# The last product of a hybrid decoder block in another order: low part of the weights first, second token block in two column halves, last squares by quarters

## The chip, the cores and the metric

One NeuronCore of a Trainium2 chip runs the kernel. The metric is the device time of one execution in microseconds (us); a comparison uses the median of several runs. Engines are named as in the profile: PE is TensorE (PEld its weight loads), DVE is VectorE, ACT is ScalarE, POOL is GpSimd, SP is SyncE. "SPq" and "ACTq" are the queues from which SP and ACT issue DMA transfers.

## What is computed

The reference takes 512 tokens of width 1024 through one block: an RMS norm, one input projection, a short gated convolution and a sliding-window attention side by side, both gated and merged, an output projection with residual, then a second norm and a squared-ReLU MLP with residual, and a last RMS norm. All of it is float32. What matters here is the end:

```python
h2 = rmsnorm(x, mlp_norm_g[l])
x = x + jnp.square(jax.nn.relu(h2 @ w_up[l])) @ w_down[l]
return rmsnorm(x, final_norm_g)      # y * rsqrt(mean(y*y) + EPS) * g
```

## The kernel before, in words

Every large product is made of float32 operands split into a high and a low part of float32r, so that one product is three: high by high, low by high and high by low. The products from the convolution's output on are done by Strassen's scheme (its Winograd form) in 12 stages. One stage (number `s`, 0 to 11) has seven unit products, in the order M1, N2, M6, M5, M7, M3, N4 (`range(7)`, line 46). In a stage that multiplies by part of `w_down` (odd `s` from 5 on; the last is `s` = 11, `STAGES - 1`), a unit product is 24 matmuls of 128 x 128 weights by 512 columns: three kinds, two blocks of 128 tokens, four slices of the contraction. `product` (line 856) issues them. As a rule it goes kind by kind; for M3 and N4 of the last stage it goes token block by token block (`by_blocks`), so that the first block is complete early.

For each unit ACT rounds the weights to their high part (`high_part`, line 1155 on, instruction on line 1164, semaphore `m_hi`) and the activations to theirs (`s_high`, line 1189, semaphore `s_hi`). DVE subtracts to get the low parts (`low_part`, line 1698, semaphore `m_lo`; `s_low`, line 1705, semaphore `s_lo`). DVE also adds each finished product from PSUM (`pair`) to the residual stream `res` in SBUF: `drain` (line 1746), and for single token blocks `drain_n4` (line 1754) and `drain_last_m3` (line 1762). PE counts its finished blocks in `prod`, DVE its additions in `drained`.

The last RMS norm is done by token block `b` (0 to 3) and column half `ch`. The half that is complete first (`early(b)`: columns 0 to 511 for blocks 0 and 1, columns 512 to 1023 for blocks 2 and 3) has its squares summed by `early_squares` and is multiplied by the gain vector `gfin`, by POOL for blocks 0 and 1 (line 621) and by DVE for blocks 2 and 3 (`gain`, line 2017). ACT forms mean + EPS of the early halves of all four blocks in one instruction (line 1402, into `rms3[:, 0, :]`). `root_of(b)` then sums the squares of the late half (line 1312, with an instruction that reads the accumulator behind it) and takes the root with that value as its bias (line 1410). DVE takes the reciprocal (`factor(b)`, line 2010), scales the late half with the gain (`scale_late(b)`, line 2024), and ACT scales the early half (`scale_early(b)`, line 1420), except that of block 2, which DVE scales (line 2096). SP issues seven stores of 256 KB in a fixed order (line 545), ACT the eighth (line 1431).

All engines work through lists written out by hand. On DVE the list ends: the low parts of M3, the addition of M7, `drain_last_m3(0)`, `s_low` and `low_part` of N4, `drain_last_m3(1)`, `factor(0)`, `scale_late(0)`, `drain_n4(0)`, `gain(2)`, `factor(1)`, `scale_late(1)`, `gain(3)`, `drain_n4(1)`, `factor(2)`, `scale_late(2)`, the early half of block 2, `factor(3)`, `scale_late(3)`. On ACT: `root_of(0)`, `root_of(1)`, `scale_early(0)`, `root_of(2)`, `scale_early(1)`, `root_of(3)`, `scale_early(3)`, the store. POOL ends with its two gain multiplications.

Of the kernel before, what the change touches and what calls it, by code (L numbers as in the profile page):

```python
# [9 lines left out]
ALU = mybir.AluOpType  # L10
ACT = mybir.ActivationFunctionType

P = 128
# [164 lines left out]
def build(nc, x, attn_norm_g, w_in, conv_w, w_conv_out, attn_sinks, rel_bias, w_attn_out, w_o,  # L178
          mlp_norm_g, w_up, w_down, final_norm_g, out):
    ctx = ExitStack()  # L180
    with ctx:
# [124 lines left out]
        def sem(name):  # L306
            return ctx.enter_context(nc.semaphore(name))
# [40 lines left out]
        passed = sem("passed")  # L348
        root_done, root3_part, root3_done = sem("root_done"), sem("root3_part"), sem("root3_done")
        ss3_ready, fin_step = sem("ss3_ready"), sem("fin_step")  # L350
        gained, gained_late = sem("gained"), sem("gained_late")
        out_early, out_late = [sem(f"out_early{b}") for b in range(TB)], sem("out_late")

        def wait(eng, s, value):
# [203 lines left out]
        @block.gpsimd  # L558
        def _(pool):
            g = nc.gpsimd  # L560
            g.memset(ident[:, :], 0.0).then_inc(ident_step, 1)
            g.memset(eps[:, :], EPS).then_inc(ident_step, 1)
            pool.wait_ge(ident_step, 2)
            g.affine_select(out=ident[:, :], in_=ident[:, :], compare_op=ALU.not_equal, fill=1.0, base=0,
                            pattern=[[-1, P]], channel_multiplier=1).then_inc(ident_step, 1)

            pool.wait_ge(x_in[TB - 1], 16)
            with nc.allow_non_contiguous_dma("a table of 32 x 16"):
                pool.dma_start(rbt[:, :], rel_bias.rearrange("b h -> h b")).then_inc(table_in, 16)
            pool.dma_start(sink[:, :], bass.AP(attn_sinks.tensor, 0, [[0, P], [1, HEADS]])).then_inc(table_in, 16)  # L570

            g.memset(ext[:, :], NEG).then_inc(ext_step, 1)
            pool.wait_ge(table_in, 16 * 2)
            pool.wait_ge(ext_step, 1)
            bucket = t5_bucket(np.arange(WINDOW))
            for b in range(BUCKETS):
                dist = np.flatnonzero(bucket == b)
                m0, n = 2 * P - 1 - int(dist[-1]), len(dist)
                g.tensor_copy(ext[:, m0:m0 + n], rbt[:, b:b + 1].to_broadcast([HEADS, n])).then_inc(ext_step, 1)


            for t in (tz[:, :, 0:2],):
                g.memset(t, 0.0).then_inc(zeroed, 1)

            for k in range(4):
                pool.wait_ge(hs_ready, k + 1)
                for part, t in enumerate((hs_hi[k], hs_lo[k])):
                    pool.dma_start(h_sums[k, part, :, :], f32(t[:, :, :]).rearrange("p k n -> p (k n)")
                                   ).then_inc(hs_out, 16)

            def mask(n, qd):


                for part, done in enumerate((pt_hi, pt_ready)):
                    pool.wait_ge(done, 4 * n + qd + 1)
                    g.affine_select(out=pt[:, part, 0, :], in_=pt[:, part, 1, :], compare_op=ALU.is_ge, fill=0.0, base=-P,
                                    pattern=[[0, 4], [1, P]], channel_multiplier=1).then_inc(pt_masked, 1)

            for n in range(1, TB):
                for qd in range(QUADS if n < TB - 1 else QUADS - 1):  # L600
                    mask(n, qd)

            for s in range(STAGES):
                pool.wait_ge(b12_in, 16 * (s + 1))
                pool.dma_start(home_rows(home_of(s, "T3")), weights(s, 1, 1), accum_op=ALU.add).then_inc(t3_in, 16)
                if s in (0, 3):
                    wait_strip(pool, S_OUT - 1 if s == 0 else S_OUT + 2)
                else:
                    wait_used(pool, s - 1, M7)
                pool.dma_start(home_rows(home_of(s, "T1")), weights(s, 0, 0)).then_inc(t1_base, 16)  # L610
                if s == 0:
                    mask(TB - 1, QUADS - 1)
                pool.wait_ge(t1_base, 16 * (s + 1))
                pool.dma_start(home_rows(home_of(s, "T1")), weights(s, 0, 1), accum_op=ALU.add).then_inc(t1_in, 16)

            def gain(b):

                pool.wait_ge(ss3_ready, b + 1)
                ch = early(b)
                r = res[:, b, 512 * ch:512 * ch + 512]  # L620
                g.tensor_tensor(r, r, gfin[:, 512 * ch:512 * ch + 512], ALU.mult).then_inc(gained, 1)

            pool.wait_ge(gfin_in, 16)
            gain(0)
            gain(1)
        N_ZEROED = 1


        @block.tensor
        def _(pe):  # L630
# [187 lines left out]
            def up_product(s, i, fresh, between=None):  # L818
# [10 lines left out]
                for kind in range(3):  # L829
# [23 lines left out]
                    if between and kind == between[0]:  # L853
                        between[1]()

            def product(s, i, fresh, between=None):

                n, thi, tlo = weight_parts(s, i)
                slot = slot_of(s, i)
                shi, slo = s_hi_tile[slot], s_lo_tile[slot]  # L860
                parts = [(shi, thi), (slo, thi), (shi, tlo)]
                order = [(b, kind) for b in range(2) for kind in range(3)] if by_blocks(s, i) else \
                    [(b, kind) for kind in range(3) for b in range(2)]
                for at_, (b, kind) in enumerate(order):
                    if b == 0:
                        if kind == 0:
                            pe.wait_ge(m_hi, n + 1)
                            pe.wait_ge(s_hi, part_no(s, i) + 1)
                        elif kind == 1:
                            pe.wait_ge(s_lo, part_no(s, i) + 1)  # L870
                        else:
                            pe.wait_ge(m_lo, n + 1)
                    a_, w = parts[kind]
                    for k in range(4):
                        last = mm(pair[region(s, i)][:, b, :], a_[:, k, b * P:(b + 1) * P], w[:, k, :],  # L875
                                  start=(fresh and kind == 0 and k == 0), stop=(kind == 2 and k == 3),
                                  skip_group_check=True)
                    if kind == 2:
                        last.then_inc(prod, 1)
                    if between and at_ == between[0]:  # L880
                        between[1]()
# [105 lines left out]
        def _(act):  # L987
# [417 lines left out]
            def root_of(b):  # L1405
# [4 lines left out]
                a(rms3[:, 1, b:b + 1], ss3[:, 1, b:b + 1], ACT.Sqrt, bias=rms3[:, 0, b:b + 1],  # L1410
                  scale=1.0 / D).then_inc(root3_done, 1)

            def scale_early(b):
                if b < 2:
                    act.wait_ge(gained, b + 1)
                else:
                    act.wait_ge(gained_late, b - 1)
                act.wait_ge(fin_step, b + 1)
                ch = early(b)
                a(res[:, b, 512 * ch:512 * ch + 512], res[:, b, 512 * ch:512 * ch + 512], ACT.Copy,  # L1420
                  scale=rms3[:, 2, b:b + 1]).then_inc(out_early[b], 1)
# [3 lines left out]
            scale_early(0)  # L1425
            root_of(2)
            scale_early(1)
            root_of(3)
            scale_early(3)
            act.wait_ge(out_early[3], 1)  # L1430
            act.dma_start(out[3 * P:TB * P, 512:D], res[:, 3, 512:D]).then_inc(out_done, 16)
# [3 lines left out]
        def _(dve):  # L1435
# [312 lines left out]
            def drain_n4(s, b):  # L1748
# [4 lines left out]
                r = res[:, 2 + b, 0:512]  # L1753
                v.tensor_tensor(r, r, pair[region(s, N4)][:, b, :], ALU.add).then_inc(drained, 1)

            def drain_last_m3(b):

                s = STAGES - 1
                dve.wait_ge(prod, 14 * s + 2 * M3 + b + 1)
                dve.wait_ge(drained, drained_before(s) + 5 + b)  # L1760
                r = res[:, b, 512:D]
                v.tensor_tensor(r, r, pair[region(s, M3)][:, b, :], ALU.add).then_inc(drained, 1)
# [244 lines left out]
            def factor(b):  # L2007

                dve.wait_ge(root3_done, b + 1)
                v.reciprocal(rms3[:, 2, b:b + 1], rms3[:, 1, b:b + 1]).then_inc(fin_step, 1)  # L2010
# [16 lines left out]
            for s in range(4, STAGES, 2):  # L2027
# [42 lines left out]
                low_part(s + 1, M3)  # L2070
                drain(s + 1, 3 + more, 1, 1, M7, ALU.subtract)
                if last:
                    drain_last_m3(0)
                s_low(s + 1, N4)
                low_part(s + 1, N4)
                if last:
                    drain_last_m3(1)
                else:
                    sum_t2(s + 2)
                    drain(s + 1, 4 + more, 0, 1, M3, ALU.add)  # L2080
                    low_part(s + 2, M1)
                    sum_t4(s + 2)

            factor(0)
            dve.wait_ge(gfin_in, 16)
            scale_late(0)
            drain_n4(STAGES - 1, 0)
            gain(2)
            factor(1)
            scale_late(1)  # L2090
            gain(3)
            drain_n4(STAGES - 1, 1)
            factor(2)
            scale_late(2)
            dve.wait_ge(gained_late, 1)
            v.tensor_scalar(res[:, 2, 512:D], res[:, 2, 512:D], rms3[:, 2, 2:3], None, ALU.mult).then_inc(out_early[2], 1)
            factor(3)
            scale_late(3)

# [21 lines left out]
```

## Time and profile before

| | us |
|---|---|
| median of 3 runs | 763.53 |
| lowest and highest | 763.16, 763.73 |
| the profiled execution's own time | 763.45 |
| its span, from the first to the last instruction | 761.7 |
| granted TensorE clock, mean | 0.998 of full speed |

The span is what the rows of the profile cover; 1.75 us of the profiled execution lie around it. In a timeline a row is the start in us, the duration in us, the engine, the line, the operation, output and input, their sizes, and how many instructions were merged; in brackets the idle time before it and what ended it. The rows of one engine overlap a little: an instruction starts some 0.08 us before the end that is recorded for the one ahead.

### The profile page before, as it was taken

The numbers are of one execution on the slowest core, as the hardware profiler recorded it, in microseconds if no ns is written. First come the engines' busy times: TensorE is split into PE (matmuls) and PEld (weight loads), VectorE is DVE, ScalarE is ACT, GpSimd is POOL, SyncE is SP. The second block draws the span as 40 slices with busy tenths as digits, with TensorE's granted clock in tenths as the row PEclk, the third lists the DMA queues.
The fourth block names the chain that finished last, engine by engine and source line by source line (L and its number), as shares of the span: only waits on it lengthen the run. The fifth ranks groups of instructions, "written<-read, shape, count | busy, mean of one in ns | idle before, by whom it ended". The sixth has DMA issues, their size and how long they took to land.

```text
span 761.7 us, 11518 instructions
## 1 busy us (share of the span) xinstructions
PE 752.7 (99%) x4563; PEld 675.0 (89%) x4563; DVE 637.4 (84%) x752; ACT 407.6 (54%) x529; POOL 75.9 (10%) x113
## 2 busy tenths in 40 slices
PE   8999999999999999999999999999999999999996
PEld 7888888888888999999988899889998999899985
DVE  5766688889896979886869899998799869986997
ACT  7424554453644655636616786654555356445565
POOL 3201000101112001010010101010101000010102
PEclk9999999999999999999999999999999999999999
DMA  7727313131219876779736866777676767777702
GB/s 255 244 83 278 111 55 111 56 111 55 72 39 262 242 186 169 194 237 327 235 80 198 219 160 173 174 205 177 175 209 172 215 166 190 196 184 203 194 1 111
DMA packets 70451, 128.13 MB, mean 168 GB/s; under 512 B 2620, under 2 KB 26244, under 8 KB 70404
## 3 DMA queue, kind: packets, MB, share of 16 engines
q1 hardware_dynamic: 53040, 85.23, 33.8%
q0 software_dynamic: 17152, 41.96, 25.4%
q8 instruction: 34, 0.56, 0.3%
q10 hardware_dynamic: 212, 0.28, 0.1%
q14 instruction: 13, 0.11, 0.0%
HBM read 121.14 MB, written 6.32 MB: 167 GB/s over the span
## 4 chain that ended last, share of the span: by engine, by line
PE 97%; DVE 1%; DMA 1%; ACT 0%; issue 0%; SPq 0%; ACTq 0%; DVEq 0%
PE pair L848 37%; PE pair L875 24%; PE pair L651 10%; PE pair L653 10%; PE pair L652 10%; PE pair L698 2%; PE pair L673 1%; PE pair L672 1%; PE pair L682 1%; DMA xn<-in_x 1%; PE pair L744 1%; PE pair L746 0%; PE pair L745 0%; PE pair L800 0%; DVE home_lo L1698 0%
## 5 line engine op out<-in xcount | busy, mean ns | idle before, releaser
L1164 ACT ACTIVATE high<-home_raw 128x2048 fp32r<-128x2048 f32 x84 | 160.9, 1916 | 156.2 <-PE pair L848 88.7
L1698 DVE TENSOR_TENSOR home_lo<-home_raw,high 128x2048 fp32r<-128x2048 f32 x84 | 192.2, 2288 | 35.3 <-ACT high L1164 34.7
L651 PE MATMUL pair<-h,wgt 128*128 128x512 f32 x320 | 126.7, 396 | 0.0
L653 PE MATMUL pair<-h,wgt 128*128 128x512 f32 x320 | 124.9, 390 | 0.0
L652 PE MATMUL pair<-h,wgt 128*128 128x512 f32 x320 | 124.8, 390 | 0.0
L653 PEld LDWEIGHTS pair<-h,wgt 128*128 128x128 f32 x320 | 60.1, 188 | 13.0
L652 PEld LDWEIGHTS pair<-h,wgt 128*128 128x128 f32 x320 | 60.3, 188 | 11.5
L651 PEld LDWEIGHTS pair<-h,wgt 128*128 128x128 f32 x320 | 60.2, 188 | 11.5
L875 PE MATMUL pair<-high,s_hi_tile 128*128 128x512 f32 x280 | 70.1, 391 | 0.0
L875 PE MATMUL pair<-home_lo,s_hi_tile 128*128 128x512 f32 x280 | 69.7, 390 | 0.0
L875 PE MATMUL pair<-high,s_lo_tile 128*128 128x512 f32 x280 | 69.7, 389 | 0.0
L875 PEld LDWEIGHTS pair<-high,s_lo_tile 128*128 128x128 f32 x280 | 52.6, 188 | 11.0
L875 PEld LDWEIGHTS pair<-home_lo,s_hi_tile 128*128 128x128 f32 x280 | 52.6, 188 | 10.9
L875 PEld LDWEIGHTS pair<-high,s_hi_tile 128*128 128x128 f32 x280 | 52.1, 188 | 10.5
L848 PE MATMUL pair<-h_hi,home_lo 128*128 128x256 f32 x448 | 58.4, 284 | 0.0
L848 PE MATMUL pair<-h_lo,high 128*128 128x256 f32 x448 | 58.4, 284 | 0.0
L848 PE MATMUL pair<-h_hi,high 128*128 128x256 f32 x448 | 58.3, 283 | 0.0
L848 PEld LDWEIGHTS pair<-h_hi,high 128*128 128x128 f32 x448 | 56.0, 192 | 0.3
L848 PEld LDWEIGHTS pair<-h_lo,high 128*128 128x128 f32 x448 | 55.7, 192 | 0.0
L848 PEld LDWEIGHTS pair<-h_hi,home_lo 128*128 128x128 f32 x448 | 55.7, 192 | 0.0
L1443 DVE TENSOR_TENSOR wgt<-raw,wgt 128x1024 fp32r<-128x1024 f32 x41 | 48.4, 1221 | 8.6 <-ACT wgt L1005 8.4
L1005 ACT ACTIVATE wgt<-raw 128x1024 fp32r<-128x1024 f32 x41 | 41.2, 1054 | 23.3 <-PE pair L653 23.1
(222 smaller groups left out, 1151.8 us busy)
## 6 DMA issues: line engine op xcount, KB each, us to landing
raw<-in_w_in SPq DMA_DIRECT2D x42, 512.0 KB, 4.8
home_raw<-in_w_up SPq DMA_DIRECT2D x16, 1024.0 KB, 5.5
home_raw<-in_w_down SPq DMA_DIRECT2D x16, 1024.0 KB, 5.1
home_raw<-in_w_up POOLq DMA_DIRECT2D x12, 1024.0 KB, 8.4
home_raw<-in_w_down POOLq DMA_DIRECT2D x12, 1024.0 KB, 8.5
home_raw<-in_w_conv_out SPq DMA_DIRECT2D x4, 1024.0 KB, 8.2
home_raw<-in_w_attn_out SPq DMA_DIRECT2D x4, 1024.0 KB, 5.2
home_raw<-in_w_in SPq DMA_DIRECT2D x4, 1024.0 KB, 5.4
```

Source lines behind the costliest of these rows:

```text
L651: mm(bank[j][:, :], wh, rhs[:, 0, k, :], start=(k == 0), stop=False)
L652: mm(bank[j][:, :], wh, rhs[:, 1, k, :], start=False, stop=False)
L653: last = mm(bank[j][:, :], wl, rhs[:, 0, k, :], start=False, stop=(k == KT - 1))
L672: mm(acc, q, khi[:, kg, keys], start=True, stop=False)
L673: last = mm(acc, q, klo[:, kg, keys], start=False, stop=True)
L698: last = mm(bank[B_PV][:, :], vs[:, kb, kg, :, :].rearrange("p a d -> p (a d)"), pt[:, part, kb, :], start=(e == 0), stop=(e == len(steps) ...
L848: last = mm(acc[:, f, :], w[:, k, f * P:(f + 1) * P], a_[:, k, :], start=(fresh and kind == 0 and k == 0 and f % 2 == 0), stop=(kind == 2 ...
L875: last = mm(pair[region(s, i)][:, b, :], a_[:, k, b * P:(b + 1) * P], w[:, k, :], start=(fresh and kind == 0 and k == 0), stop=(kind == 2 ...
L1005: a(wgt[weight_slot(s1)][:, 0, 1024 * e:1024 * e + 1024], raw[raw_slot(c1)][:, :], ACT.Copy).then_inc(hi_ready, 1)
L1164: a(high[n % 2][:, :], home_raw[home_of(s, name)][:, :], ACT.Copy).then_inc(m_hi, 1)
L1443: v.tensor_tensor(w[:, 1, 1024 * e:1024 * e + 1024], raw[raw_slot(2 * s1 + e)][:, :], f32(w[:, 0, 1024 * e:1024 * e + 1024]), ALU.subtract ...
L1698: v.tensor_tensor(home_lo[home][:, :], home_raw[home][:, :], f32(high[n % 2][:, :]), ALU.subtract).then_inc(m_lo, 1)
```

## The change

It touches the last unit product (N4 of stage 11) and what follows it. On PE, `product` hands that unit to a new function: token block 0 is done in the order high by high, high by low part of the weights, low by high; token block 1 is done in two halves of 256 columns, each with all three kinds, the second half into a PSUM bank of its own (`pair[0]`), from zero. On DVE, `low_part(N4)` moves ahead of `drain_last_m3(0)` and `s_low(N4)`; the last addition becomes two (`drain_last`, 512 columns, then 256 columns of the other bank); `factor(1)` and `gain(2)` stand ahead of `drain_n4(0)`, `factor(2)` ahead of the first last addition, `gain(3)` between the two, `scale_late(2)` behind them; the scaling of block 2's early half goes to ACT. On ACT the last squares are summed over 256 columns twice, the first sum into a scratch column; POOL divides that by 1024 and adds it to the bias, and the last root waits for POOL.

```diff
@@ block.gpsimd
             gain(0)
             gain(1)
+            pool.wait_ge(ss3_ready, TB + 4)
+            pool.wait_ge(root3_part, 1)
+            g.tensor_scalar(rms3[:, 2, 3:4], rms3[:, 2, 3:4], 1.0 / D, None, ALU.mult).then_inc(bias_step, 1)
+            pool.wait_ge(bias_step, 1)
+            g.tensor_tensor(rms3[:, 0, 3:4], rms3[:, 0, 3:4], rms3[:, 2, 3:4], ALU.add).then_inc(bias_last, 1)
@@ block.tensor
+            def last_product():
+                s, i = STAGES - 1, N4
+                n, thi, tlo = weight_parts(s, i)
+                shi, slo = s_hi_tile[slot_of(s, i)], s_lo_tile[slot_of(s, i)]
+                acc = pair[region(s, i)]
+                pe.wait_ge(m_hi, n + 1)
+                pe.wait_ge(s_hi, part_no(s, i) + 1)
+                for k in range(4):
+                    mm(acc[:, 0, :], shi[:, k, 0:P], thi[:, k, :], start=False, stop=False, skip_group_check=True)
+                pe.wait_ge(m_lo, n + 1)
+                for k in range(4):
+                    mm(acc[:, 0, :], shi[:, k, 0:P], tlo[:, k, :], start=False, stop=False, skip_group_check=True)
+                pe.wait_ge(s_lo, part_no(s, i) + 1)
+                for k in range(4):
+                    last = mm(acc[:, 0, :], slo[:, k, 0:P], thi[:, k, :], start=False, stop=(k == 3),
+                              skip_group_check=True)
+                last.then_inc(prod, 1)
+                for ch in range(2):
+                    c = cols(2 * P * ch, 2 * P)
+                    half = pair[0][:, 0, 0:2 * P] if ch else acc[:, 1, c]
+                    for a_, w in ((shi, thi), (shi, tlo), (slo, thi)):
+                        for k in range(4):
+                            last = mm(half, a_[:, k, P:2 * P], w[:, k, c], start=(ch == 1 and k == 0 and a_ is shi and w is thi),
+                                      stop=(a_ is slo and k == 3), skip_group_check=True)
+                    last.then_inc(prod, 1)
@@ product
+                if s == STAGES - 1 and i == N4:
+                    last_product()
+                    return
@@ block.scalar
+            def last_squares(ch):
+                act.wait_ge(drained, drained_before(STAGES - 1) + 9 + ch)
+                act.wait_ge(ss3_ready, TB + 3 + ch)
+                a(tz[:, 0, 0:256], res[:, 3, 256 * ch:256 * ch + 256], ACT.Square,
+                  accum_out=(rms3[:, 2, 3:4], ss3[:, 1, 3:4])[ch]).then_inc(ss3_ready, 1)
...
             scale_early(1)
-            root_of(3)
+            scale_early(2)
+            last_squares(0)
+            last_squares(1)
+            act.wait_ge(bias_last, 1)
+            act.wait_ge(ss3_ready, TB + 5)
+            a(rms3[:, 1, 3:4], ss3[:, 1, 3:4], ACT.Sqrt, bias=rms3[:, 0, 3:4], scale=1.0 / D).then_inc(root3_done, 1)
             scale_early(3)
@@ block.vector
+            def drain_last(ch):
+                s = STAGES - 1
+                dve.wait_ge(prod, 14 * s + 2 * N4 + 2 + ch)
+                dve.wait_ge(drained, drained_before(s) + 8 + ch)
+                r = res[:, 3, 256 * ch:512]
+                p = pair[0][:, 0, 0:256] if ch else pair[region(s, N4)][:, 1, :]
+                v.tensor_tensor(r, r, p, ALU.add).then_inc(drained, 1)
...
                 if last:
+                    low_part(s + 1, N4)
                     drain_last_m3(0)
-                s_low(s + 1, N4)
-                low_part(s + 1, N4)
-                if last:
+                    s_low(s + 1, N4)
                     drain_last_m3(1)
                 else:
+                    s_low(s + 1, N4)
+                    low_part(s + 1, N4)
...
             scale_late(0)
+            factor(1)
+            gain(2)
             drain_n4(STAGES - 1, 0)
-            gain(2)
-            factor(1)
             scale_late(1)
+            factor(2)
+            drain_last(0)
             gain(3)
-            drain_n4(STAGES - 1, 1)
-            factor(2)
+            drain_last(1)
             scale_late(2)
-            dve.wait_ge(gained_late, 1)
-            v.tensor_scalar(res[:, 2, 512:D], res[:, 2, 512:D], rms3[:, 2, 2:3], None, ALU.mult).then_inc(out_early[2], 1)
             factor(3)
             scale_late(3)
```

## Rows read from the trace of the kernel before

**Rows 1.** The page: busy time by engine, and the chain's shares.

```profile
PE 752.7 (99%) x4563; PEld 675.0 (89%) x4563; DVE 637.4 (84%) x752; ACT 407.6 (54%) x529; POOL 75.9 (10%) x113
...
PE 97%; DVE 1%; DMA 1%; ACT 0%; issue 0%; SPq 0%; ACTq 0%; DVEq 0%
```

**Rows 2.** Busy time by stretch: window, length, PE PEld DVE ACT POOL, clock, DMA.

```profile
750.00:755.00 5.00, 5.00 (x23) 4.09 (x22) 4.84 (x8) 3.21 (x11) 0.00 (x0) 1.00 0.20 75
```

**Rows 3.** The chain that ended last, in its last ten us: start, us, what.

```profile
753.00 0.68 DVE res L1754
...
757.77 0.72 ACT res L1420
```

**Rows 4.** Timeline of PE, two stretches of merged matmuls.

```profile
700.01 2.08 PE L848 MATMUL pair<-h_hi,high 128*128 128x256 f32 x16
701.93 2.08 PE L848 MATMUL pair<-h_lo,high 128*128 128x256 f32 x16
...
751.77 1.10 PE L875 MATMUL pair<-home_lo,s_hi_tile 128*128 128x512 f32 x4
...
754.55 1.07 PE L875 MATMUL pair<-home_lo,s_hi_tile 128*128 128x512 f32 x4
```

**Rows 5.** Timeline of DVE, from 743 us to the end.

```profile
743.52 2.29 DVE L1698 TENSOR_TENSOR home_lo<-home_raw,high 128x2048 fp32r<-128x2048 f32 x1
745.72 1.22 DVE L1746 TENSOR_TENSOR res<-res,pair 128x1024 f32<-128x1024 f32 x1
747.43 0.69 DVE L1762 TENSOR_TENSOR res<-res,pair 128x512 f32<-128x512 f32 x1 [0.49 <-PE pair L875]
748.04 1.30 DVE L1705 TENSOR_TENSOR s_lo_tile<-hid,s_hi_tile 128x1024 fp32r<-128x1024 f32 x1
749.26 2.28 DVE L1698 TENSOR_TENSOR home_lo<-home_raw,high 128x2048 fp32r<-128x2048 f32 x1
751.46 0.67 DVE L1762 TENSOR_TENSOR res<-res,pair 128x512 f32<-128x512 f32 x1
...
752.33 0.75 DVE L2024 SCALAR_TENSOR_TENSOR res<-res,rms,gfin 128x512 f32<-128x512 f32 x1
...
755.06 0.68 DVE L2017 TENSOR_TENSOR res<-res,gfin 128x512 f32<-128x512 f32 x1
755.66 0.68 DVE L1754 TENSOR_TENSOR res<-res,pair 128x512 f32<-128x512 f32 x1
...
757.51 0.16 DVE L2010 RECIPROCAL rms<-rms 128x1 f32<-128x1 f32 x1
```

**Rows 6.** Timeline of ACT: squares and root of block 2.

```profile
753.74 0.62 ACT L1312 ACTIVATE tz<-res 128x512 f32<-128x512 f32 x1
...
754.48 0.29 ACT L1410 ACTIVATE rms<-ss,rms 128x1 f32<-128x1 f32 x1
```

**Rows 7.** Two lines alone: count, ns min/median/max, first and last start.

```profile
L621 POOL TENSOR_TENSOR res<-res,gfin x2: 1310/2674/4037, 743.0 to 746.9; 128x512 f32<-128x512 f32 x2
...
L1705 DVE TENSOR_TENSOR s_lo_tile<-hid,s_hi_tile x20: 1214/1222/1299, 466.9 to 748.0; 128x1024 fp32r<-128x1024 f32 x20
```

**Rows 8.** Timeline at 16 us and at 131 us, POOL and DVE.

```profile
16.03 1.27 POOL L579 COPY ext<-rbt 16x1 f32<-16x1 f32 x1
16.04 1.22 DVE L1443 TENSOR_TENSOR wgt<-raw,wgt 128x1024 fp32r<-128x1024 f32 x1
...
131.23 1.01 POOL L596 TENSOR_SCALAR_AFFINE_SELECT pt<-pt 128x512 fp32r<-128x512 f32 x1 [59.62 <-ACT pt L1090]
131.90 0.88 DVE L1615 SCALAR_TENSOR_TENSOR ty<-tz,pcol,ty 128x512 f32<-128x512 f32 x1 [0.15 <-DVE ty L1615]
```

**Rows 9.** Small POOL instructions: one in the timeline, one line's durations.

```profile
1.29 0.29 POOL L564 TENSOR_SCALAR_AFFINE_SELECT ident<-ident 128x128 f32<-128x128 f32 x1 [0.23 <-POOL eps L562]
...
L579 POOL COPY ext<-rbt x32: 173/176/2448, 15.9 to 23.1; 16x1 f32<-16x1 f32 x16, 16x3 f32<-16x3 f32 x3, 16x4 f32<-16x4 f32 x2, 16x6 f32<-16x6 f32 x2
```

**Rows 10.** Timeline: the last store.

```profile
758.52 0.39 ACTq L1431 DMA_DIRECT2D out<-res  x1
```

More of the change, by code:

```diff
@@ L350, in build @@
         ss3_ready, fin_step = sem("ss3_ready"), sem("fin_step")
-        gained, gained_late = sem("gained"), sem("gained_late")
+        gained, gained_late, bias_step, bias_last = (sem(n) for n in ("gained", "gained_late", "bias_step", "bias_last"))
         out_early, out_late = [sem(f"out_early{b}") for b in range(TB)], sem("out_late")
```

## The prediction

> **What bounds the kernel now.** I read the page first: PE is busy for 752.7 us of a span of 761.7, and the chain that ended last is 97% PE [rows 1]. The windows come next: the clock is granted in full at the end too, and PE is busy all through 750 to 755 [rows 2]. So nothing is to be had ahead of the last product; what the change can move is the tail. The chain has it: from 753.00 it leaves PE, runs over DVE's additions and gains, and ends with ACT's scaling of block 3 at 757.77 [rows 3]. Its last store is issued at 758.52 and the span ends 3.2 us later [rows 10]. The last matmuls end at 754.55 + 1.07 = 755.62 [rows 4]. Then comes a serial piece: last addition 755.66, reciprocal 757.51, store 758.52 [rows 5, 10].
>
> I measure from the profiled execution: 763.45 us, 0.08 under the median of 763.53, with 1.75 us around its span. 0.2% is 1.53 us, about what a measurement of this kernel can tell from no change; faster means under 762.0, slower over 765.06.
>
> **PE's part.** The low part of N4's weights is ready at 749.26 + 2.28 = 751.54 [rows 5] and the matmuls that need it start at 751.77 [rows 4]. With that part made first this wait goes, but it is worth 0.05 us at most. The halves double 12 matmuls of block 1 to 24. Sixteen matmuls of 256 columns follow each other in 701.93 - 700.01 = 1.92 us, so 0.12 us each [rows 4]; 24 take 2.88 us. The 12 of block 1 take 2.72 to 2.75 us (751.77 to 754.55 is 12 matmuls, a wait and all: 2.78) [rows 4]. PE thus ends 0.1 to 0.2 us later, near 755.8, and its first half is ready near 754.3. Neither decides, as follows.
>
> **DVE's list up to block 1.** DVE's instructions start 0.08 us before the recorded end of the one ahead, when nothing is waited for. The addition of M7 ends at 746.94 [rows 5]; now `low_part(N4)` follows at 746.86 (before, DVE stood idle for 0.49 us until PE had M3's first block [rows 5]) and ends at 749.15. `drain_last_m3(0)` runs from 749.07 and `s_low(N4)` from 749.67. By durations alone it would end at 750.9, and `drain_last_m3(1)` would start 0.6 us earlier than its 751.46 [rows 5].
>
> But POOL is at its gain multiplications. The first is recorded from 743.0 for 4.04 us, the second from 746.9 for 1.31 [rows 7]: the first got nowhere until DVE's subtraction of two SBUF operands ended at 745.81 [rows 5], then took the 1.2 us that the second took, beside additions from PSUM. The same holds for the smallest instructions: a copy of 16 x 1, 0.18 us as a rule [rows 9], took 1.27 us beside a DVE subtraction of two SBUF operands of 1.22 [rows 8]. And it holds the other way round: a DVE instruction of two SBUF operands that came while POOL was at work took 0.88 us [rows 8] where its like takes 0.75 [rows 5], and `s_low(N4)`, met by the last 0.2 us of POOL's second gain, took 1.30 where the median is 1.22 [rows 7]. So each waits for the other's whole instruction. After the change POOL's second gain is held by `low_part(N4)` to 749.15, works to 750.35, and holds `s_low(N4)`: started at 749.67, it gets its data some 0.5 us late and ends near 751.4. PE wants that part at 751.5; it just holds. `drain_last_m3(1)` starts at 751.35: of 0.6 us, 0.1 remains.
>
> The Trainium skill has this as a rule (SBUF — State Buffer, section on its two separate sides): DVE and GpSimd share a port pair that is locked for a full instruction, against DVE when it has two SBUF inputs, and the first to start has it. The rows agree, 1.27 for 0.18. It speaks against this change twice; without it the sum below would be about +0.4 us instead of +1.4.
>
> **From there to the last addition.** `factor(1)` and `gain(2)` now stand ahead of `drain_n4(0)`, and `factor(1)` waits for ACT's root of block 1. From the end of an addition to the end of the root it takes 0.06 + 1.03 us (753.68 to 754.77, by the squares at 753.74 and the root at 754.48 with 0.29 [rows 3, 6]), and 0.09 more to the reciprocal. So: `drain_last_m3(1)` ends 752.03, root 753.12, `factor(1)` 753.2, `gain(2)` 753.3, and 0.60 later (as 755.06 to 755.66 [rows 5]) `drain_n4(0)` at 753.9, where it was 753.00 [rows 3]. Behind it on DVE waits all the rest. `scale_late(1)` fits in beside ACT's root of block 2, which ends at 754.58 + 1.09 = 755.67; `factor(2)` 755.76, again a wait in the middle of the list. Then `drain_last(0)` at 755.85, `gain(3)` 756.45, `drain_last(1)` 757.05. PE had both halves by 755.8: the queue is late, not PE. The width of 256 columns costs 0.41 us (0.68 for 512 less half of the 0.54 between 512 and 1024 [rows 5]), so the last addition ends at 757.46 instead of 755.66 + 0.68 = 756.34: +1.12 us.
>
> **The last root.** Squares of 512 columns took 0.74 us to the root's start (753.74 to 754.48 [rows 6]). For 256 I take 0.53, as if ACT's columns cost what DVE's do or a little less: -0.22 us. The first quarter's squares are beside DVE's work and end near 757.3 (ACT now also scales block 2's early half, 0.72 us [rows 3], ending near 756.9, still ahead). Then POOL: two instructions of one column. No row shows them; the nearest are 0.18 us for a copy and 0.23 between two that wait for each other [rows 9]. Woken 0.2 us after 757.3, POOL finds `scale_late(2)` on DVE, two SBUF operands, from 757.38 to 758.13. Held, its first ends near 758.2, the second near 758.6, and the root starts at 758.67 instead of 758.03: +0.64. Bounds: 0 if POOL is let through between (0.6 us for both then fits beside the second quarter, save 0.1), +0.9 if each costs the 0.29 of the wider one [rows 9] and waking it takes as long again. I take +0.64.
>
> **After it** nothing is changed: reciprocal, two scalings, two stores. SP's store of block 2's late half comes out at 758.2 instead of near 757.3, the next behind it; two issues of 0.4 us [rows 10] are over by 759.1, before block 3 is ready. The last two stores meet fewer others, worth 0 to 0.3: I take -0.1.
>
> **Sum:** +1.12 - 0.22 + 0.64 - 0.1 = +1.44: 763.45 + 1.44 = 764.9 us.
>
> **Rivals.** (a) The forecast, two holds of the port: 764.9, of its own 764.3 to 765.3. Chance 0.55. (b) The port costs little: POOL's second gain or its bias slips between. Without the first hold -0.45, without the second -0.64: 763.8 to 764.4. For it: DVE's additions from PSUM leave gaps. Against: the holds in rows 7 and 8. Chance 0.23. (c) Slower: at 747.0 POOL's second gain gets the port ahead of `low_part(N4)`, which came at 746.86 while the first still worked. Then that part starts 1.2 us late and ends at 750.4, still in time for PE; `s_low` ends 752.1, PE waits 0.6 us, and the whole list stands 0.6 to 0.7 us later: 765.5. It decides as soon as `low_part(N4)` lasts over 2.6 us. For it: POOL's two gains follow without a gap. Against: at 16.04 DVE came into a run of POOL copies and was not delayed [rows 8]. Chance 0.18. (d) The tail has no waits: if the two roots hold up none of the work on DVE, the last addition starts when PE is done, at 755.8, and is 0.27 shorter, squares -0.22, and the time is 763.1. Against: both `factor` calls stand in the queue ahead. Chance 0.04. That it goes under 762.0 would need PE's matmuls to end earlier than they can.
>
> **How the numbers follow.** The likeliest is 764.9. Over 765.06 lie (c) and about a quarter of (a): 0.18 + 0.15 = 0.33. Under 762.0: 0.01 to 0.02. The range goes from the lower part of (b), 763.7, to (c) with its own spread, 765.8.
>
> **What would show it.** `s_low(N4)` of about 1.7 us; idle time of DVE ahead of `factor(1)` and `factor(2)`, ended by ACT; the last addition over 1 us behind PE's last matmul; POOL's first bias instruction far longer than 0.2 us, ending with `scale_late(2)`; ACT's last root waiting for POOL. Wrong would be: `drain_n4(0)` before 753.3, or a root that waits for its own squares alone.

## The result and the profile after

| | before | after |
|---|---|---|
| median, us (21 runs each) | 763.16 | 764.34 |
| lowest and highest | 762.46, 763.85 | 763.71, 765.11 |
| profiled execution, its span | 763.45, 761.7 | 763.79, 762.1 |

The ratio is 1.0014, interval 1.0008 to 1.002: 1.2 us slower. The interval does not hold 1, and it ends at 0.2%, the line that the prediction drew between "slower" and "no change". The prediction said 764.9, a rise of 1.44 us over the 763.45 that it started from.

The two profiled executions differ by 0.34 us only. Runs of one kernel spread over 1.4 us, and in the profiles most of the spread lies ahead of the part that was changed: POOL starts its first gain multiplication at 742.28 us of the span after the change, at 742.96 before it, and at 742.28 to 743.31 over all thirteen traces. So I read the tail from that start, ahead of which no edit here changes the work, to the issue of ACT's store. Before it is 758.52 - 742.96 = 15.56 us [rows 10], after it 758.98 - 742.28 = 16.70: +1.14 us, close to the 1.18 between the medians. To lay a time of after beside one of before, add 0.68.

(In the text ahead, the unit numbers stand on line 38 and `high_part` begins on line 1150. After the change DVE's lines are 48 to 57 higher: 1698 is 1746, 1705 is 1753, 1754 is 1802, 2010 is 2067.)

The timeline of DVE after the change, from the last unit product's low parts on:

```profile
746.18 2.29 DVE L1746 TENSOR_TENSOR home_lo<-home_raw,high 128x2048 fp32r<-128x2048 f32 x1
748.38 0.68 DVE L1819 TENSOR_TENSOR res<-res,pair 128x512 f32<-128x512 f32 x1
748.98 1.72 DVE L1753 TENSOR_TENSOR s_lo_tile<-hid,s_hi_tile 128x1024 fp32r<-128x1024 f32 x1
750.62 0.68 DVE L1819 TENSOR_TENSOR res<-res,pair 128x512 f32<-128x512 f32 x1
...
752.42 0.17 DVE L2067 RECIPROCAL rms<-rms 128x1 f32<-128x1 f32 x1 [0.17 <-ACT rms L1446]
752.50 0.67 DVE L2074 TENSOR_TENSOR res<-res,gfin 128x512 f32<-128x512 f32 x1
753.09 0.68 DVE L1802 TENSOR_TENSOR res<-res,pair 128x512 f32<-128x512 f32 x1
753.69 0.75 DVE L2081 SCALAR_TENSOR_TENSOR res<-res,rms,gfin 128x512 f32<-128x512 f32 x1
754.89 0.16 DVE L2067 RECIPROCAL rms<-rms 128x1 f32<-128x1 f32 x1 [0.45 <-ACT rms L1446]
754.97 0.69 DVE L1811 TENSOR_TENSOR res<-res,pair 128x512 f32<-128x512 f32 x1
755.57 0.68 DVE L2074 TENSOR_TENSOR res<-res,gfin 128x512 f32<-128x512 f32 x1
756.17 0.41 DVE L1811 TENSOR_TENSOR res<-res,pair 128x256 f32<-128x256 f32 x1
756.50 0.75 DVE L2081 SCALAR_TENSOR_TENSOR res<-res,rms,gfin 128x512 f32<-128x512 f32 x1
```

Against rows 5, `s_low` (third line) takes 1.72 us where it took 1.30, two reciprocals now have idle time before them (0.17 and 0.45 us, ended by ACT's roots), and the last addition ends at 756.58, which is 757.26 on the scale of before, where it was 756.34. What PE, ACT and POOL do behind that, from the same timeline:

```profile
754.39 0.64 PE L885 MATMUL pair<-high,s_lo_tile 128*128 128x256 f32 x4
...
755.99 0.40 ACT L1453 ACTIVATE tz<-res 128x256 f32<-128x256 f32 x1
...
756.57 0.77 POOL L628 TENSOR_SCALAR rms<-rms 128x1 f32<-128x1 f32 x1 [6.95 <-ACT tz L1453]
756.62 0.42 ACT L1453 ACTIVATE tz<-res 128x256 f32<-128x256 f32 x1
756.94 0.19 ACT L1453 ACTIVATION_READ_ACCUMULATOR tz<-res 128x1 f32 x1
757.42 0.19 POOL L630 TENSOR_TENSOR rms<-rms 128x1 f32<-128x1 f32 x1
757.64 0.29 ACT L1476 ACTIVATE rms<-ss,rms 128x1 f32<-128x1 f32 x1 [0.52 <-POOL rms L630]
...
758.98 0.39 ACTq L1479 DMA_DIRECT2D out<-res  x1
```

PE's last matmuls end at 755.03; the last addition starts 1.14 us later, where before it followed within 0.04 us [rows 4, 5]. POOL's first bias instruction, one column, takes 0.77 us and ends 0.09 us behind DVE's scaling that began at 756.50. The chain of waits, which before had only DVE and, at its end, ACT here [rows 3], now goes over POOL:

```profile
755.37 0.71 ACT res L1463
756.08 0.41 ACT tz L1453 x2
756.49 0.08 issue
756.57 0.77 POOL rms L628
757.34 0.04 issue
757.38 0.24 POOLq L181
757.62 0.02 issue
757.64 0.30 ACT rms L1476
```

### The profile page after: what moved, and what is told of

It reads as the page before. It is cut to its first block, busy times and chain, and to the rows that moved or that the text cites. A ratio compares the mean times of both kernels' runs of the same rounds, so it can differ in the third digit from the quotient of the medians.

```text
span 762.1 us, 11552 instructions
## 1 busy us (share of the span) xinstructions
PE 753.0 (99%) x4575; PEld 676.1 (89%) x4575; DVE 638.0 (84%) x752; ACT 408.3 (54%) x532; POOL 79.1 (10%) x115
## 4 chain that ended last, share of the span: by engine, by line
PE 91%; DVE 4%; issue 2%; ACT 2%; DMA 0%; POOL 0%; POOLq 0%; ACTq 0%
PE pair L853 36%; PE pair L911 20%; PE pair L656 10%; PE pair L658 10%; PE pair L657 10%; PE pair L703 2%; DVE home_lo L1746 1%; PE pair L678 1%; PE pair L677 1%; PE pair L687 1%; DVE res L1794 1%; PE pair L749 1%; ACT high L1200 1%; DMA xn<-in_x 0%; PE pair L750 0%
## 5 line engine op out<-in xcount | busy, mean ns | idle before, releaser
L911 PE MATMUL pair<-high,s_hi_tile 128*128 128x512 f32 x272 | 67.9, 391 | 0.0
L911 PE MATMUL pair<-high,s_lo_tile 128*128 128x512 f32 x272 | 67.5, 389 | 0.0
L911 PE MATMUL pair<-home_lo,s_hi_tile 128*128 128x512 f32 x272 | 67.5, 389 | 0.0
```

## The experiments

The tail is measured in each one's profile, as above; the medians come from 10 or 11 runs each, beside runs of the kernel before on the same chip.

| | tail, us | median, us | before, us | ratio (interval) |
|---|---|---|---|---|
| before | 15.56 | 763.16 | | |
| after | 16.70 | 764.34 | 763.16 | 1.0014 (1.0008 to 1.002) |
| e1: POOL's second gain later | 16.33 | 763.9 | 763.26 | 1.0006 (0.9997 to 1.0015) |
| e2: bias by ACT | 16.37 | 764.16 | 763.26 | 1.001 (1.0001 to 1.0019) |
| e3: DVE's old list | 16.07 | 763.69 | 763.26 | 1.0005 (0.9996 to 1.0014) |
| e4: no halves, no quarters | 16.09 | 763.64 | 763.26 | 1.0006 (0.9997 to 1.0015) |
| e5: old list, bias by DVE | 16.18 | 763.99 | 763.32 | 1.0008 (0.9999 to 1.0017) |
| e6: low part first alone | 15.50 | 763.0 | 763.32 | 0.9996 (0.9987 to 1.0005) |
| e7: rearranged | 15.26 | 762.95 | 763.32 | 0.9995 (0.9986 to 1.0004) |
| e8: old front | 16.87 | 764.52 | 763.32 | 1.0015 (1.0006 to 1.0024) |
| e9: e5, ACT scales block 2 | 16.31 | 763.63 | 763.06 | 1.0005 (0.9996 to 1.0015) |
| e10: e6, first step of the list | 15.53 | 763.13 | 763.06 | 1.0 (0.999 to 1.0009) |
| e11: e6, second step | 15.45 | 762.89 | 763.06 | 0.9996 (0.9987 to 1.0006) |

Only after, e2 and e8 lie clear of before in time. The verdicts on mechanisms below rest on the profiles' rows, one profile for each kernel. The same piece comes out alike in them: `s_low`, where it meets POOL's second gain as it does after the change, took 1.72 to 1.74 us in all ten traces. A tail difference of a few hundredths of a microsecond is still not to be read as a gain or a loss.

**e1, POOL's second gain later.**

```diff
             gain(0)
+            pool.wait_ge(s_lo, part_no(STAGES - 1, N4) + 1)
             gain(1)
```

> The changed kernel, but POOL's second gain multiplication waits until the low part of N4's activations is made. I measure the tail from the start of POOL's first gain to the issue of ACT's store: 15.56 us before, 16.70 after the change. Theory (a shared port, held for a whole instruction): s_low(N4) takes 1.22 us instead of 1.72, the last addition of M3 starts 0.5 us earlier, and as the list behind it hangs on ACT's roots, all of it moves: tail 16.2 to 16.3 us, time 0.4 to 0.5 us less. Rival (s_low is slow for another reason, or the list is set by PE): tail 16.7 us, nothing gained.

```profile
749.78 1.22 DVE L1754 TENSOR_TENSOR s_lo_tile<-hid,s_hi_tile 128x1024 fp32r<-128x1024 f32 x1
...
751.08 1.31 POOL L621 TENSOR_TENSOR res<-res,gfin 128x512 f32<-128x512 f32 x1 [3.98 <-DVE s_lo_tile L1754]
751.51 0.16 DVE L2068 RECIPROCAL rms<-rms 128x1 f32<-128x1 f32 x1
...
751.79 1.15 DVE L2082 SCALAR_TENSOR_TENSOR res<-res,rms,gfin 128x512 f32<-128x512 f32 x1
```

`s_low` is back at 1.22 us, and the hold has moved to where POOL now works: `scale_late(0)`, 0.75 us elsewhere, takes 1.15. The tail is 0.37 us shorter. So a DVE instruction with two SBUF operands loses time while POOL is at work: POOL's gain takes the 1.31 us that it took where nothing met it, DVE's scaling ends 0.55 us behind it (752.94 and 752.39), and moving POOL's work moves the loss.

**e2, the bias by ACT** (POOL's two instructions taken out).

```diff
             last_squares(0)
+            act.wait_ge(ss3_ready, TB + 4)
+            a(rms3[:, 0, 3:4], rms3[:, 2, 3:4], ACT.Identity, bias=rms3[:, 0, 3:4], scale=1.0 / D).then_inc(bias_last, 1)
             last_squares(1)
```

> The changed kernel, but the last bias is made by one ACT instruction of one column between the two quarters of squares; POOL has nothing to do there. Theory (POOL's first bias instruction is held by DVE's scaling of block 2): the root waits only for its own squares, which start 0.1 us later: tail 16.3 us instead of 16.70. Rival (the root waits for its squares anyhow, POOL is hidden): tail 16.8 us.

Tail 16.37: the root waits for its own squares alone. They start 0.1 us later, as expected, and 0.33 us are won in all. The rival, a root that waits for its squares anyhow, is refuted.

**e3, DVE's old list behind `scale_late(0)`**, halves, quarters and POOL's bias kept; ACT's `scale_early(2)` goes, as DVE does it again.

```diff
-            factor(1)
-            gain(2)
             drain_n4(STAGES - 1, 0)
+            gain(2)
+            factor(1)
             scale_late(1)
-            factor(2)
-            drain_last(0)
             gain(3)
+            drain_last(0)
             drain_last(1)
+            factor(2)
             scale_late(2)
+            dve.wait_ge(gained_late, 1)
+            v.tensor_scalar(res[:, 2, 512:D], res[:, 2, 512:D], rms3[:, 2, 2:3], None, ALU.mult).then_inc(out_early[2], 1)
```

> The changed kernel with DVE's list behind scale_late(0) in its old order (block 2's addition before the reciprocal of block 1, the reciprocal of block 2 behind the last additions, block 2's early half scaled by DVE), the two halves, the quarters and POOL's bias kept. Theory (the reciprocals in front make DVE wait for ACT's roots): block 2's addition 0.8 us earlier, no idle time of DVE before the reciprocals, the last addition 0.6 us earlier. POOL's bias then meets two scalings of DVE and may be held to the end of both, which gives back 0.2 to 0.6 us: tail 16.3 to 16.7 us. Rival (PE sets the last addition): last addition at the same distance from PE's end as after the change, 1.1 us.

```profile
756.62 0.23 POOL L628 TENSOR_SCALAR rms<-rms 128x1 f32<-128x1 f32 x1 [6.56 <-ACT tz L1453]
756.63 0.42 ACT L1453 ACTIVATE tz<-res 128x256 f32<-128x256 f32 x1
756.63 0.75 DVE L2080 SCALAR_TENSOR_TENSOR res<-res,rms,gfin 128x512 f32<-128x512 f32 x1
756.94 0.48 POOL L630 TENSOR_TENSOR rms<-rms 128x1 f32<-128x1 f32 x1
757.30 0.48 DVE L2154 TENSOR_SCALAR res<-res,rms 128x512 f32<-128x512 f32 x1
757.46 0.29 ACT L1475 ACTIVATE rms<-ss,rms 128x1 f32<-128x1 f32 x1 [0.33 <-POOL rms L630]
```

Tail 16.07, below the 16.3 to 16.7 that was expected, for a reason that the rows show. POOL's first bias instruction starts 0.01 us ahead of DVE's scaling and takes 0.23 us; the second, which took 0.19 us after the change, starts beside it and takes 0.48, until DVE is done. So neither instruction is slow by itself, nor is the first one slow because it is the first of its kind: the one that starts while DVE's scaling is running is.

**e4, no halves and no quarters.** Block 1 as 12 matmuls of 512 columns, `drain_n4(1)` behind `gain(3)`, `root_of(3)`, no bias by POOL; the new list kept.

```diff
-            drain_last(0)
             gain(3)
-            drain_last(1)
+            drain_n4(STAGES - 1, 1)
```

> The changed kernel without column halves and without quarters: block 1 in 12 matmuls of 512 columns, one last addition, whole squares, root with its old bias, no POOL work; the new order of DVE's list and the low part first are kept. Theory (halves and quarters pay nothing where DVE is late, and POOL's bias costs 0.5 us): last addition ends at the same place as after the change, squares 0.2 us longer, no wait for POOL: tail 16.1 us. Rival (the halves do bring the last squares forward): tail 16.9 us or more.

```profile
755.56 0.68 DVE L1790 TENSOR_TENSOR res<-res,pair 128x512 f32<-128x512 f32 x1
756.27 0.63 ACT L1340 ACTIVATE tz<-res 128x512 f32<-128x512 f32 x1 [0.19 <-DVE res L1790]
```

Tail 16.09 as expected. The last addition ends 13.96 us behind POOL's first gain (after the change: 14.30), the root starts at 14.75 (after: 15.36). Halves, quarters and POOL's bias together cost 0.61 us.

**e8, the old front** in the changed kernel (PE takes the low part of the activations second and that of the weights third again, to match).

```diff
-                    low_part(s + 1, N4)
                     drain_last_m3(0)
                     s_low(s + 1, N4)
+                    low_part(s + 1, N4)
                     drain_last_m3(1)
```

> The changed kernel with the first part of the change undone on DVE and PE (s_low before the low part of the weights, PE's order to match), the rest kept. Theory: s_low(N4) back at 1.3 us, but the low part of the weights now stands ahead of block 1's M3 addition, which comes 0.15 us later than after the change; DVE's waits for the roots pass that on: tail 16.85 us. Rival (the hold of s_low is a loss against the order before): tail 16.2 us.

Tail 16.87, expected 16.85. Behind the new list the first part of the change gains 0.17 us although `s_low` is held for 0.5 us: M3's second addition starts 8.51 us behind POOL's first gain here, 8.34 after the change.

**e6, the low part first alone:** e4 with the old list, so that only PE's order and these lines differ from the kernel before.

```diff
+                    low_part(s + 1, N4)
                     drain_last_m3(0)
                     s_low(s + 1, N4)
-                    low_part(s + 1, N4)
                     drain_last_m3(1)
```

> The kernel before with the first part of the change alone: the low part of N4's weights first on DVE and PE. Theory: harmless, since the last additions wait for PE: tail 15.5 us, though s_low(N4) takes 1.7 us here too. Rival (the hold of s_low by POOL costs time wherever it occurs): tail 16.0 us.

```profile
749.21 1.73 DVE L1740 TENSOR_TENSOR s_lo_tile<-hid,s_hi_tile 128x1024 fp32r<-128x1024 f32 x1
...
755.15 0.69 DVE L1789 TENSOR_TENSOR res<-res,pair 128x512 f32<-128x512 f32 x1
```

Tail 15.50: the hold is there (1.73 us) and costs nothing, since PE's last matmuls end at 755.11 and the last addition starts 0.04 us behind. Taken in this order the 1.14 us divide so: low part first -0.06, the new list with ACT's scaling +0.59 (15.50 to 16.09), halves, quarters and POOL's bias +0.61 (16.09 to 16.70). Such steps always add up, so the other order is the test: by e3 halves, quarters and POOL's bias come to +0.57 (15.50 to 16.07) and the list to +0.63 (16.07 to 16.70). The two parts hardly depend on each other. In the list's part ACT's scaling costs nothing: in e4 ACT stands idle for 0.19 us between it and the squares.

**e10 and e11, one step of the new list each,** on e6.

```diff
 e10
+            factor(1)
+            gain(2)
             drain_n4(STAGES - 1, 0)
-            gain(2)
-            factor(1)
 e11
             scale_late(1)
+            factor(2)
             gain(3)
             drain_n4(STAGES - 1, 1)
-            factor(2)
```

> The run with the low part first (tail 15.50 us), and of the new list only the first step: reciprocal of block 1 and gain of block 2 ahead of block 2's addition. Theory (only idle time of DVE costs, and here it is 0.2 us, most of it slack before the last addition, which waits for PE): block 2's addition 0.9 us later, last addition within 0.1 us of where it was, tail 15.5 to 15.6 us. Rival, the step as the prediction put it (the 0.9 us is passed on to the end): tail 16.4 us.

> The run with the low part first (tail 15.50 us), and of the new list only the second step: reciprocal of block 2 ahead of block 3's gain and last addition. Theory: with block 2's addition early, its root is ready when the reciprocal's turn comes, so DVE does not wait: last addition 0.1 us later, tail 15.6 us. Only both steps together, as in the change, make the 0.45 us of waiting. Rival (a reciprocal in front of an addition costs wherever it stands): tail 15.9 us or more.

Of e10:

```profile
753.21 0.16 DVE L2054 RECIPROCAL rms<-rms 128x1 f32<-128x1 f32 x1 [0.17 <-ACT rms L1438]
...
753.88 0.68 DVE L1789 TENSOR_TENSOR res<-res,pair 128x512 f32<-128x512 f32 x1
...
755.74 0.68 DVE L1789 TENSOR_TENSOR res<-res,pair 128x512 f32<-128x512 f32 x1
```

With its first gain at 743.07, block 2's addition starts at 10.81 us and the last one at 12.67; in e6 they start at 9.92 and 12.64. The 0.89 us by which the first is late is gone but for 0.03 by the second: DVE had `gain(2)` done instead. Only 0.17 us were idle. Against that, the last addition no longer waits some 0.05 us for PE, and the reciprocal takes 0.08 us of the list in front of a gain where it takes 0.19 in front of the scaling that needs it (753.21 to 753.29 here, 753.64 to 753.83 in e6). In e11 (tail 15.45, expected 15.6) DVE has no idle time ahead of the reciprocals of blocks 1 and 2, as the root of block 2 is ready in time. It takes both steps: a late addition of block 2 and, behind it, a reciprocal that needs its root before the last addition. That is the 0.45 us ahead of the second reciprocal of after and of e4.

**e5 and e9, two misses.** e5 is e3 with the bias by one DVE instruction behind the last addition and POOL's two instructions taken out. e9 is e5 with `factor(2)` behind `scale_late(1)` and block 2's early half scaled by ACT between the two quarters.

```diff
             drain_last(1)
+            dve.wait_ge(ss3_ready, TB + 4)
+            v.scalar_tensor_tensor(out=rms3[:, 0, 3:4], in0=rms3[:, 2, 3:4], scalar=1.0 / D, in1=rms3[:, 0, 3:4],
+                                   op0=ALU.mult, op1=ALU.add).then_inc(bias_last, 1)
...
 e9, on ACT
             last_squares(0)
+            scale_early(2)
             last_squares(1)
```

> The run with DVE's old list, halves and quarters kept, but the last bias made by one DVE instruction of one column behind the last addition, none by POOL. Tail as before from POOL's first gain to ACT's store: 15.56 us before the change, 16.70 after, 16.07 with the old list and POOL's bias. Theory: the root then waits for its own squares alone: tail 15.8 us. What is left against before (0.2 us) is the second addition, which stands behind the first on DVE although PE was done. Rival (the halves and quarters do pay once POOL is out of the way): 15.4 us or less.

> The run with the old list and the bias on DVE came out at a tail of 16.18 us where 15.8 was expected; its profile has the last root done at 14.8 us behind POOL's first gain and the reciprocal only at 15.18, behind DVE's scaling of block 2's early half. Here that scaling goes to ACT, between the two quarters of squares, and the reciprocal of block 2 stands behind scale_late(1), where its root is ready. Theory (DVE has more work than time there): the reciprocal follows its root at once, tail 15.8 to 15.9 us. Rival (ACT's squares are late for another reason): tail 16.1 us or more.

e5 has a tail of 16.18 where 15.8 was expected, no better than with POOL. The rows say why:

```profile
757.38 0.29 ACT L1470 ACTIVATE rms<-ss,rms 128x1 f32<-128x1 f32 x1
757.65 0.48 DVE L2152 TENSOR_SCALAR res<-res,rms 128x512 f32<-128x512 f32 x1
758.05 0.15 DVE L2061 RECIPROCAL rms<-rms 128x1 f32<-128x1 f32 x1
```

The root is done at 757.67, but DVE is still busy and takes the reciprocal 0.38 us late; where POOL was awaited, that work was hidden. In e9 the reciprocal does follow its root at once, as the theory had it, but the tail is 16.31 where 15.8 to 15.9 was expected:

```profile
754.79 0.15 DVE L2062 RECIPROCAL rms<-rms 128x1 f32<-128x1 f32 x1
...
756.17 0.42 ACT L1448 ACTIVATE tz<-res 128x256 f32<-128x256 f32 x1 [1.06 <-DVE res L1806]
...
756.59 0.71 ACT L1458 ACTIVATE res<-res,rms 128x512 f32<-128x512 f32 x1
757.20 0.40 ACT L1448 ACTIVATE tz<-res 128x256 f32<-128x256 f32 x1
```

ACT's scaling from 756.59 holds the second quarter's squares up to 757.20, half a microsecond behind e5's. That is a matter of its place and not of a full list: ACT stood idle for 1.06 us ahead of the first quarter, and the scaling's inputs were ready once the reciprocal of block 2 was done at 754.94. Ahead of the first quarter, where the change has it, its 0.71 us would have fitted into that gap. By these rows it would save some 0.4 us, for a tail near 15.9; that is an estimate and was not run.

**e7, rearranged by these findings.** Low part first, halves and quarters kept; `drain_n4(0)` ahead of `factor(1)`; `gain(2)` to POOL; bias by DVE; ACT scales block 2's early half between the quarters.

```diff
             scale_late(0)
-            factor(1)
-            gain(2)
             drain_n4(STAGES - 1, 0)
+            factor(1)
             scale_late(1)
-            factor(2)
             drain_last(0)
+            factor(2)
             gain(3)
             drain_last(1)
+            dve.wait_ge(ss3_ready, TB + 4)
+            v.scalar_tensor_tensor(out=rms3[:, 0, 3:4], in0=rms3[:, 2, 3:4], scalar=1.0 / D, in1=rms3[:, 0, 3:4],
+                                   op0=ALU.mult, op1=ALU.add).then_inc(bias_last, 1)
```

> What the findings point to: low part first, halves and quarters kept; block 2's addition ahead of both reciprocals that wait for ACT, the gain of block 2 given to POOL behind its second, bias by one DVE instruction, ACT scaling block 2's early half between the two quarters. Theory (DVE's list is the bound from 752 us on, each 512-wide operation taken out or no longer behind a wait is worth its 0.6 us until PE's end sets the pace): tail 15.3 to 15.4 us, just under before. Rival (POOL's third gain holds DVE's scalings as long as it saves): tail 15.8 us or more.

```profile
751.99 0.91 DVE L2077 SCALAR_TENSOR_TENSOR res<-res,rms,gfin 128x512 f32<-128x512 f32 x1
...
755.56 0.42 DVE L1807 TENSOR_TENSOR res<-res,pair 128x256 f32<-128x256 f32 x1
```

Tail 15.26, the shortest: the last addition starts at 12.78 us, close behind PE, as halves need it, and POOL's third gain costs DVE 0.16 us once (0.91 for 0.75). What the halves themselves give here isn't shown, as this list was not run without them. Its median is 0.37 us under before, but the ratio's interval (0.9986 to 1.0004) holds 1: the profile shows 0.3 us, the medians can't tell it from no change.

## Why the prediction was right

The direction, the size and the two holds came out. The time is 0.56 us under the forecast of 764.9. Half of that is the starting point, 763.45 of one execution where the median of 21 is 763.16; the other half is the rise, forecast as +1.44 and measured as +1.18. Luck has a share in this: by its time alone, 764.34 fits rival (b) (763.8 to 764.4) as well as (a) (764.3 to 765.3). The rows decide for (a). By its steps, its times on the scale of before, after's with 0.68 added:

- **DVE's list up to block 1.** `s_low` was forecast at about 1.7 us and took 1.72; `drain_last_m3(1)` at 751.35, measured 751.30. e1 shows that POOL's second gain is the cause. "It just holds" was too tight: PE came to that part at 751.77, not at 751.5, 0.39 us behind the end of `s_low`. By the Trainium skill (SBUF — State Buffer, section on its two separate sides) the side that starts first has the shared port for its whole instruction. Rows of e1 (POOL 0.71 us ahead, DVE held) and the second bias instruction of e3 (DVE 0.31 us ahead, POOL held) agree; for starts within 0.05 us of each other see the last section.
- **From there to the last addition.** `drain_n4(0)` forecast 753.9, measured 753.77; last addition's end 757.46, measured 757.26. The path holds: late addition of block 2, late root, `factor(2)` waiting for it, last additions behind. The term was 0.20 us too large, mostly because a reciprocal starts 0.03 to 0.04 us behind the end of its root and not 0.09. But "behind it on DVE waits all the rest", said of `drain_n4(0)` alone, is wrong: e10 has that same delay of block 2's addition and loses 0.03 us of tail. What costs is idle time of DVE, 0.17 + 0.45 us, and it needs both reciprocals ahead (e10, e11). The prediction had summed positions and so got the sum nearly right.
- **The last root.** Forecast +0.64 for POOL, measured 0.48: the squares' last record ends at 757.13 and the root starts at 757.64, where 0.03 us lay between in the old `root_of` (0.09 in e2, e5 and e7, which sum by quarters but don't wait for POOL, so that POOL's own share is 0.42). The term was too large mostly by the pause between POOL's two instructions: 0.08 us (757.34 to 757.42), not the 0.23 of rows 9. With ACT in its place 0.33 us come back (e2).
- **Halves and quarters.** The forecast gave +1.12 to the end of the last addition and -0.22 for the squares without telling list from halves. e4 does: the second addition adds 0.34 us, the shorter squares give 0.22 back, and POOL's wait makes the rest of 0.61.
- **PE's part.** 24 matmuls of 256 columns ran from 752.00 to 755.03; the 12 of 512 columns in e4, whose block 1 starts at 752.00 too, end at 754.88, 0.15 us earlier. It decided nothing, as said.
- **After it.** From the last store's issue to the end of the span 3.18 us before and 762.1 - 758.98 = 3.12 after: -0.06, taken as -0.1. The spans are given to 0.1 us, so no run tells this term from nothing. Ahead of that store 0.05 us came back, which the forecast left out: the last reciprocal starts 0.33 us behind its root's start, before 0.38, as DVE no longer has block 2's early half to scale.

Rival (b) named a slip of POOL past the port; it happened in e3 (first bias instruction, 0.23 us), not here. Rival (c), POOL first at 747.0, did not: `low_part(N4)` took 2.29 us, its usual time, and had started some 0.1 us ahead of POOL's second gain (746.18 and 746.3). Rival (d) is refuted by the 1.14 us between PE's end and the last addition.

## What to carry to other kernels

Splitting the last piece of work did not help here, since the engine that takes it over was late already; look at how far behind PE that engine is before cutting PE's work finer. In a list written by hand, an operation that waits for another engine's result costs what it idles, not where it stands; two such waits in a row, the second fed by something the first delayed, are the pattern to look for. And work given to POOL is not done beside DVE's if DVE is then in an instruction with two SBUF operands: the smallest piece, 0.23 us by itself, took 0.77 us here, as long as that one.

## What was not expected of the hardware

Two dependent POOL instructions of one column follow each other in 0.08 to 0.09 us and take 0.19 to 0.23 us each when nothing holds them. Who gets the port when both ask at once can't be told from recorded starts: at 16.03 POOL was 0.01 us ahead of DVE and was held for 1.27 us [rows 8]; in e3 it was 0.01 us ahead and went through in 0.23. And a waiting POOL was not let in between two DVE instructions with two SBUF operands that follow each other: its first gain waits through the end of one and all of the next, to 745.81 [rows 5, 7], and takes 4.01 to 4.04 us in all thirteen traces. A small copy in the kernel before shows both, 0.05 us ahead of DVE and held through two of its subtractions:

```profile
19.76 2.45 POOL L579 COPY ext<-rbt 16x6 f32<-16x6 f32 x1
19.81 2.36 DVE L1443 TENSOR_TENSOR wgt<-raw,wgt 128x1024 fp32r<-128x1024 f32 x2
```
